# Two transformer blocks on one core: another order of calls on VectorE and ScalarE in the attention of the two layers

## What is computed

```python
for l in range(DEPTH):                      # 2 layers
    h = rms_norm(x, attn_norm_g[l])
    proj = h @ w_in[l]
    (mq, mk, mv, dq, dk, dv, sq, sk, sv, iq, ik, iw) = jnp.split(proj, offsets, axis=-1)
    ...
    _, sel = lax.top_k(score, n_top)        # n_top = 64
    ...
    x = x + mix @ w_out[l]
    x = x + (silu(h2 @ w_gate[l]) * (h2 @ w_up[l])) @ w_down[l]
```

## Time and profile before

| | |
|---|---|
| median of three runs | 1248.62 us (1248.52 to 1250.57) |
| the profiled execution's own time | 1250.09 us |
| its span, first to last instruction | 1248.4 us |
| TensorE busy | 1228.6 us, 98% of the span |
| VectorE busy | 805.0 us, 64% |
| ScalarE busy | 674.8 us, 54% |
| GpSimd busy | 204.4 us, 16% |
| mean granted TensorE clock | 0.996 |

### The profile page before, as it was taken

One profiled execution on the slowest core, in us unless ns is written; L12 is line 12 of the kernel. 1 busy time (PEld: TensorE's weight loads), 2 busy tenths in 40 slices (PEclk: granted clock), 3 DMA queues, 4 the chain that ended last, 5 costly groups with the idle time before them and its releaser, 6 DMA issues.

```text
span 1248.4 us, 16867 instructions
## 1 busy us (share of the span) xinstructions
PE 1228.6 (98%) x6398; PEld 1038.2 (83%) x6398; DVE 805.0 (64%) x959; ACT 674.8 (54%) x1015; POOL 204.4 (16%) x174
## 2 busy tenths in 40 slices
PE   8999999999999899999999999999999999999998
PEld 7778888888887888888888899888997788888886
DVE  6798654545658966545547756876685697655544
ACT  5768454443558666344446455655547755644443
POOL 5895100001179730000000000000000030000000
PEclk9999999999999999999999999999999999999999
DMA  7533455556463254555555464343334455555551
GB/s 268 192 105 120 160 212 177 193 193 207 132 219 106 93 190 152 214 196 175 200 174 192 170 233 171 130 152 129 108 124 166 169 189 183 202 199 178 192 212 41
DMA packets 32795, 212.73 MB, mean 170 GB/s; under 512 B 3777, under 2 KB 3905, under 8 KB 10082
## 3 DMA queue, kind: packets, MB, share of 16 engines
q1 hardware_dynamic: 32674, 211.82, 47.8%
q0 software_dynamic: 64, 0.13, 0.0%
HBM read 210.88 MB, written 1.05 MB: 170 GB/s over the span
## 4 chain that ended last, share of the span: by engine, by line
PE 84%; DVE 8%; ACT 3%; POOL 2%; DMA 1%; issue 1%; SPq 0%; DVEq 0%; ACTq 0%; POOLq 0%
PE bank L605 24%; PE bank L607 24%; PE bank L606 24%; PE bank L1054 2%; DVE wlo L1783 2%; ACT probs L1384 2%; PE bank L635 1%; PE bank L889 1%; PE bank L800 1%; DMA raw<-in_w_out 1%; ACT whi L1296 1%; DVE z L2266 1%; PE bank L734 1%; POOL gain L524 1%; PE bank L760 1%
## 5 line engine op out<-in xcount | busy, mean ns | idle before, releaser
L1783 DVE TENSOR_TENSOR wlo<-raw,whi 128x2048 fp32r<-128x2048 f32 (+4 forms) x197 | 444.5, 2262 | 255.1 <-ACT whi L1296 253.6
L1296 ACT ACTIVATE whi<-raw 128x2048 fp32r<-128x2048 f32 (+5 forms) x201 | 369.0, 1842 | 131.0 <-PE bank L607 123.2
L605 PE MATMUL bank<-whi,hT_hi 128*128 128x512 f32 (+4 forms) x1028 | 401.5, 391 | 4.4 <-DVE wlo L1783 4.2
L607 PE MATMUL bank<-whi,hT_lo 128*128 128x512 f32 (+4 forms) x1028 | 392.8, 382 | 0.0
L606 PE MATMUL bank<-wlo,hT_hi 128*128 128x512 f32 (+4 forms) x1028 | 392.4, 382 | 0.0
L605 PEld LDWEIGHTS bank<-whi,hT_hi 128*128 128x128 f32 x1028 | 193.9, 189 | 41.8 <-DVE wlo L1783 6.1
L607 PEld LDWEIGHTS bank<-whi,hT_lo 128*128 128x128 f32 x1028 | 193.7, 188 | 35.8
L606 PEld LDWEIGHTS bank<-wlo,hT_hi 128*128 128x128 f32 x1028 | 194.1, 189 | 32.4
L605 PE MATMUL bank<-whi,mixT_hi 128*128 128x512 f32 (+1 forms) x248 | 95.3, 384 | 0.2 <-DVE wlo L1783 0.2
L605 PE MATMUL bank<-whi,ffT_hi 128*128 128x512 f32 x240 | 93.7, 390 | 0.0
L607 PE MATMUL bank<-whi,ffT_lo 128*128 128x512 f32 x240 | 93.5, 390 | 0.0
(11 more groups left out here) (295 smaller groups left out, 1462.2 us busy)
## 6 DMA issues: line engine op xcount, KB each, us to landing
raw<-in_ff_loop SPq DMA_DIRECT2D x90, 1024.0 KB, 4.8
raw<-in_w_groups SPq DMA_DIRECT2D x64, 1024.0 KB, 4.8
raw<-in_w_out SPq DMA_DIRECT2D x8, 1024.0 KB, 5.6
raw<-in_ff_first SPq DMA_DIRECT2D x6, 1024.0 KB, 4.9
raw<-in_w_values SPq DMA_DIRECT2D x8, 728.0 KB, 4.1
raw<-in_w_comp SPq DMA_DIRECT2D x4, 1024.0 KB, 6.8
raw<-in_ff_last SPq DMA_DIRECT2D x3, 1024.0 KB, 4.8
raw<-in_w_values SPq DMA_DIRECT2D x4, 736.0 KB, 5.1
```

Source lines behind the costliest of these rows:

```text
L605: eng.matmul(out, lhsT=hi, rhs=wh, start=start, stop=False)
L607: return eng.matmul(out, lhsT=lo, rhs=wh, start=False, stop=stop)
L1296: eng.activation(whi[j][:, 0:n], raw[j][:, 0:n], ACT.Copy).then_inc(hi_ready, 1)
L1783: eng.tensor_tensor(wlo[j][:, 0:n], raw[j][:, 0:n], whi[j][:, 0:n].bitcast(F32), ALU.subtract).then_inc(lo_ready, 1)
```

## The change

Two lines of ScalarE's list and two lines of VectorE's list get another order; no call is added or taken away, and TensorE's, GpSimd's and SyncE's lists stay as they are. It applies to both layers. The lines are 1497 and 1498 for ScalarE, and 2136 and 2137 for VectorE.

On ScalarE, `attend_exp` of tile 1 and `hi(6, 0)` go ahead of `scale_heads(l, 2)`, and `hi(6, 1)` goes ahead of `copy_z(l, 5, 0)`, the squares and a heads copy. On VectorE, `lo(6, 0)` comes after two rounds of the selection where it came after five, `attend_copy` after it and not before, and `lo(6, 1)` after three rounds where it came after six.

```diff
-                scale_heads(l, 2); attend_exp(A + 0, 0, (1,)); hi(6, 0); attend_exp(A + 0, 0, (2,))
-                copy_z(l, 5, 0); square_heads(l, 3, 0); heads_copy(l, 3, 0); hi(6, 1); copy_z(l, 5, 1)
+                attend_exp(A + 0, 0, (1,)); hi(6, 0); scale_heads(l, 2); attend_exp(A + 0, 0, (2,)); hi(6, 1)
+                copy_z(l, 5, 0); square_heads(l, 3, 0); heads_copy(l, 3, 0); copy_z(l, 5, 1)
...
-                head_sums(l, 2, 1); topk_rounds(0, 4); attend_copy(A + 0); topk_rounds(4, 5)
-                lo(6, 0); topk_rounds(5, 6); lo(6, 1); head_sums(l, 3, 0); topk_rounds(6, 7); head_sums(l, 3, 1)
+                head_sums(l, 2, 1); topk_rounds(0, 2); lo(6, 0); attend_copy(A + 0); topk_rounds(2, 3)
+                lo(6, 1); topk_rounds(3, 5); head_sums(l, 3, 0); topk_rounds(5, 7); head_sums(l, 3, 1)
```

## The result

The changed kernel took 1253.17 us (median of 15 runs, 1250.89 to 1254.04) against 1249.35 us (15 runs, 1247.83 to 1251.08): ratio 1.0028, 95% interval 1.0021 to 1.0035, some 3.5 us slower. The forecast was 1250.1, range 1247.3 to 1252.6, most likely within 0.2% (0.60; slower had 0.30); it came out slower, and above the range. The profiled execution took 1253.47 us.

A forecast was written before the change was run, and what follows sets the result against it. TensorE's list of calls was taken as the path, with waits for VectorE's split and GpSimd. Layer shifts 0.6 + 0.5 = +1.1 us, or +1.9 at VectorE's floor; the middle, +1.5, gave 1250.1 us, range 1247.3 to 1252.6.

The forecast's parts named there:

- The first split: VectorE's lo(6, 0) in layer 0, meeting a GpSimd instruction: 0.74 us longer than 1.67, ending at 82.29.
- The second: VectorE's lo(6, 1) in layer 0, asked for at 84.25: 2.13 us long against 1.90 before, ending at 86.38.
- GpSimd's set: GpSimd's third set, which the turned heads need, held up by both splits: ends at 88.63, 1.27 us later.
- The wait at L971: TensorE, after six matmuls of product 6, waits for GpSimd before the turned heads: 3.1 us, until 88.7.
- that at L605: TensorE's wait of 1.98 us for VectorE's split ahead of product 6: gone in both layers.
- VectorE's longer way: VectorE's work before the first mask: 0.74 plus 0.23 us of waiting for GpSimd, free at 93.31.
- The step that failed: TensorE, turned heads to scores in layer 0: low clock stays in its old place, scores at 91.7 against 91.03.
- The stage: Interval from group 0's mask to group 1's on VectorE: the latter 0.6 us later in layer 0, 0.5 in layer 1.
- The forecast's second estimate: If faster runs have no slow stretch, VectorE's floor is the shift in each layer: 2 x 0.97 = +1.9 us.
- The slow one: Rival: TensorE's low clock lasts until the scores are done, mask at 94.7, +1.9 us a layer, 1252.4 us; chance 0.22.
- No shift: Rival: GpSimd isn't held up as counted, turned heads at or before 87.4, 1247.3 to 1248.6 us; chance 0.11.
- faster: Rival: TensorE's waits and half its low clock go whole, 7.4 us, 1241.2 us; chance 0.10, whole or over 2.5 us.

The follow-up runs named there:

- e1: Kernel before with only ScalarE's two reordered lines, VectorE as before; ratio to the kernel before 1.0004.
- e4: Changed kernel plus 30 unread identity transposes on TensorE in the wait ahead of the turned heads; ratio to the kernel before 1.0014, 1251.56 us.
- e5: Kernel before plus 18 unread identity transposes in TensorE's wait of 1.98 us ahead of product 6; ratio to the kernel before 0.9994.
- e3: Changed kernel, but the second split, lo(6, 1), stays behind the sixth selection round; ratio to the kernel before 1.0007.
- e11: e3 plus four VectorE additions over 384 columns, both inputs in SBUF, after the third selection round; one run, 1261.79 us.
- e12: e3 plus four VectorE maxima over 384 columns, one input in SBUF, after the third selection round; one run, 1256.22 us.
- e6: Changed kernel with TensorE's turned heads moved behind row_product(6, 0, 0) and group_values(0); ratio to the kernel before 1.0028.
- e13: e6 plus 20 identity transposes ahead of group_turn(1) and 16 ahead of row_product(7, 0, 0) on TensorE; ratio to the kernel before 1.0021, 1251.70 us.
- e10: e5 with VectorE's seventh selection round moved behind the first blend; ratio to the kernel before 0.9995.

## Why the prediction was wrong

**What held.** ScalarE's moves alone cost nothing that shows (e1). The first split was forecast at 2.41 us ending at 82.29; it took 2.42 and ended at 82.46, 0.16 of it from the opening. The second: forecast 2.13 and 86.38, measured 2.12 and 86.52. GpSimd's set: forecast 88.63, measured 88.77. The wait at L971: forecast 3.1, measured 3.21 and 3.19, and that at L605 went. VectorE's longer way, 0.97 a layer, is what e4 and e5 differ by. The exclusion of GpSimd's instructions and VectorE's with two inputs in SBUF, which carried all this, held in e3, e11 and e12.

**The step that failed** is the one on TensorE's clock: "From 88.7, 2.6 us lie in the slow stretch (74% of the work), the rest takes 0.46". I left the low stretch where it had been before, and as long, although the wait ahead of it had another place and was 1.2 us longer. Measured, in layer 0 the clock was low for 6.83 us and not 3.41, so that nearly all of the work up to the mask lay in it: turned heads to scores 3.72 us, scores to mask 2.68, where I had 3.0 and 1.66. In layer 1, where the stretch had its length but began later, turned heads to scores took 3.45 us, where I had 2.9. The stage grew by 2.28 and 0.92 us and not by 0.6 and 0.5, and TensorE, not VectorE, held the mask in both (waits of 1.76 and 0.46 us). This is one execution, at a mean clock of 0.995; the six runs at 0.997 and 0.998 took 1251.8 us, which lies inside the forecast's range.

**How much was the clock.** The profiled executions split the growth of both stages, 3.20 us together, as follows. Between e5 and e4, both without low clock in the stage, lie 1.93 us, VectorE's longer way. Filling the waits gives back 2.41 us of the changed kernel (e4) and 1.14 of the kernel before (e5); the difference, 1.27, is what the change's further low clock costs. The times say the same less sharply. By e4, filling the wait takes the ratio from 1.0028 to 1.0014, 1.7 us, by e5 it is worth 0.7; of the 3.5 us that makes some 1.0 for the further low clock and leaves 2.5 between e4 and e5, of which 1.9 is VectorE's way. The remaining 0.6 (1.0 without e5's three runs at 0.998) is within the error of the ratios and was not traced. The forecast's second estimate, +1.9 for runs without low clock, is thus right for VectorE's way. Taking the middle of +1.1 and +1.9 was the second error: the lower value was a shift against one execution with two low stretches, and the runs of the kernel before at clock 1.0, above, had fewer. A third part of the miss is the base: 1248.62 us was the median of three runs, and that of fifteen is 1249.35, 0.7 higher.

**The rivals.** The slow one was the outcome in layer 0, for its reason and near its price: 94.7 forecast for the mask, 95.23 measured, of it 0.16 from the opening. For layer 1 it was too dear. Its 1252.4 us stood against the earlier median, 1248.62 us; the kernel before took 1249.35 in the comparison. I gave it 0.22 and wrote as its condition that more than 3.4 us a layer be low; it needed less, in layer 1 only a stretch that begins 0.35 us ahead of the turned heads and not 1.2. "No shift" and "faster" needed GpSimd's set earlier or unhindered, and neither was.

**The price of the low clock** in the Trainium skill, its time by one less the ratio ("TensorE: Matmul & The Clock Gate", "Terms"), gives an estimate of 1.7 us for a stretch of 3.41. No stage here paid that. In the kernel before a stretch cost 0.54 and 0.60 us (e5), since VectorE was waited for from there on. In the changed kernel the one of layer 1 cost 0.54 and the 6.83 us of layer 0 cost 1.87 (e4), where the formula has 3.4; e6's 3.41 and 6.83 us cost 1.1 and 2.1 (e13). It may have been paid in full at e5's 124.95, where TensorE was busy for the whole stretch: of the delay of 3.2 us there, 1.3 is longer waiting.

## What to carry to other kernels

Before moving an instruction ahead for one engine's sake, look at what the other engines' instructions beside its new place are: here a split that came 3.4 us sooner on VectorE made a GpSimd instruction 1.3 us longer, and GpSimd was 0.26 us from being the next thing that TensorE waits for. Where a wait on TensorE is moved or lengthened, cost the matmuls behind it twice, once at the full clock and once at the low one until the next engine's wait, and not at the clock that each had in the profile. A wait that is filled or moved only pays as far as the other engines are ready earlier too.

## What the runs showed of the hardware

The low clock does not always come with a wait of the same length. Behind the same wait of 2.04 us it followed in layer 0 and not in layer 1 (e1); behind 1.90 us likewise (e3); it came behind e5's waits of 0.62 and 1.31 us too; after the 3.21 us of the changed kernel it held for 6.83 us, though TensorE was busy 2.44 of the first 3.41. What decides it was not found. With the wait filled with transposes it was 1.00 in both layers of e4 and e10, and in the stages of e5.

Of VectorE's and GpSimd's exclusion I had not expected the asymmetry: four short additions (0.55 us alone, at L1885) delayed GpSimd by 0.4 us together and took 4.87 us themselves, because each came to its end only behind a longer GpSimd instruction. The hand-over has a constant size in these traces: the one that waits ends, after the other's recorded end, by its own length less 0.14 us, VectorE's split of 1.67 us by 1.53, GpSimd's instruction of 1.04 us by 0.90, and e11's additions of 0.55 us by 0.41. The rule of the Trainium skill ("SBUF — State Buffer", "SBUF: two separate sides") has whichever began first hold for its whole instruction, be it VectorE's with two SBUF inputs or GpSimd's; e11 agrees with it, and e12, with one input, saw no meeting.
